# A two-block network's two expert routers: ranks in fewer products, modulation pieces at other places, values broadcast in row groups

## The reference

```python
def hier_moe(tokens, w1, b1, w2, b2, w_gate, w_up, w_down):
    p1 = jax.nn.softmax((tokens @ w1 + b1).astype(jnp.float32), axis=-1)
    p_grp, grp = lax.top_k(p1, 1)
    lg2 = (tokens @ w2 + b2).astype(jnp.float32).reshape(n, N_GROUPS, EXPERTS_PER_GROUP)
    lg2 = jnp.take_along_axis(lg2, grp[:, :, None], axis=1)[:, 0]
    top_val, top_idx = lax.top_k(lg2, TOP_K_INNER)
    gate = p_grp * jax.nn.softmax(top_val, axis=-1)
    expert = grp * EXPERTS_PER_GROUP + top_idx
    return grouped_experts(tokens, expert, gate.astype(tokens.dtype), w_gate, w_up, w_down)

sh1, sc1, g1, sh2, sc2, g2 = jnp.split(jax.nn.silu(cond) @ w + b, 6, axis=-1)   # the modulation, per layer
```

## Time and profile before

| | us |
|---|---|
| median of 3 runs | 2017.17 (2016.58 to 2017.70) |
| profiled execution, its own time | 2015.87 |
| its span | 2014.0 |
| TensorE busy in the span | 1789.0 (89%) |
| DVE, ACT, POOL busy | 1017.2, 418.1, 566.7 |
| read from HBM | 572.08 MB, 285 GB/s over the span |

### The profile page before, as it was taken

How to read it: one execution, slowest core, us unless ns; L and a number is a source line. 1 busy time by engine, 2 the same in 40 slices (tenths; PEclk the granted TensorE clock), 3 DMA queues, 4 the chain that set the end, 5 groups by cost and what they waited for, 6 DMA issues and landing times.

```text
span 2014.0 us, 56742 instructions
## 1 busy us (share of the span) xinstructions
PE 1789.0 (89%) x23884; PEld 1238.6 (61%) x23885; DVE 1017.2 (51%) x2416; ACT 418.1 (21%) x832; POOL 566.7 (28%) x431
## 2 busy tenths in 40 slices
PE   7999989999999987898988967667669989999998
PEld 4444466666666654645776745445447777788887
DVE  3798156677666656346345633333246995210001
ACT  2001242212211214115341211111113224210001
POOL 0000026777766761001033522222248000100000
PEclk9999989999999998999989987887888889999999
DMA  9854168899999999822169999999996255433320
GB/s 369 310 205 167 42 233 351 340 422 429 427 430 429 427 430 396 294 84 74 43 249 429 417 428 428 429 428 429 429 413 236 101 217 202 167 126 126 126 105 21
DMA packets 109379, 574.33 MB, mean 285 GB/s; under 512 B 4976, under 2 KB 10224, under 8 KB 84592
## 3 DMA queue, kind: packets, MB, share of 16 engines
q1 hardware_dynamic: 108720, 570.72, 70.7%
q10 hardware_dynamic: 576, 2.43, 0.3%
HBM read 572.08 MB, written 1.05 MB: 285 GB/s over the span
## 4 chain that ended last, share of the span: by engine, by line
PE 62%; DMA 26%; DVE 6%; issue 2%; ACT 2%; SPq 2%; DVEq 0%; ACTq 0%
PE bank L349 24%; PE bank L554 14%; DMA ring<-in_expert_w_gate 11%; DMA ring<-in_expert_w_down 7%; DMA ring<-in_expert_w_up 6%; PE bank L526 4%; PE bank L974 4%; PE bank L508 3%; PE bank L601 3%; DVE b L1034 2%; ACT b L1847 2%; DMA ring<-in_conv_w_in 1%; PE bank L890 1%; PE bank L420 1%; DMA ring<-in_attn_w_in 1%
## 5 line engine op out<-in xcount | busy, mean ns | idle before, releaser
L554 PE MATMUL bank<-ring,b 128*32 128x128 f32 (+1 forms) x13600 | 521.0, 310 | 133.7 <-DMA ring<-in_expert_w_gate 75.3
L554 PEld LDWEIGHTS bank<-ring,b 128*32 128x32 f32 x13600 | 402.3, 116 | 305.4 <-issue 155.1
L1034 DVE TENSOR_TENSOR h_t<-h_t,bank 128x512 f32<-128x512 f32 (+1 forms) x696 | 349.9, 564 | 316.6 <-PE bank L526 316.6
L349 PE MATMUL bank<-h_t,ring 128*128 128x256 f32 (+1 forms) x1600 | 424.0, 427 | 5.2 <-ACT h_t L1847 2.5
L1847 ACT ACTIVATE b<-bank 128x256 f32<-128x256 f32 (+4 forms) x371 | 142.8, 400 | 1298.0 <-PE bank L554 749.5
L349 PEld LDWEIGHTS bank<-h_t,ring 128*128 128x128 f32 x1600 | 306.9, 193 | 116.5 <-issue 77.4
L2269 POOL TENSOR_SCALAR b<-b 128x1024 f32<-128x1024 f32 (+1 forms) x85 | 195.1, 2295 | 46.0 <-POOL b L2277 33.6
L2277 POOL TENSOR_TENSOR b<-b 128x512 f32<-128x512 f32 (+1 forms) x85 | 88.8, 1045 | 411.5 <-PE bank L526 411.5
L526 PE MATMUL bank<-b 32*128 32x512 f32 (+1 forms) x1392 | 172.3, 565 | 5.4 <-DVE h_t L1034 4.7
L1034 DVE TENSOR_TENSOR b<-b,bank 128x128 f32<-128x128 f32 (+3 forms) x124 | 49.9, 406 | 234.4 <-PE bank L349 155.0
L2272 POOL TENSOR_TENSOR b<-b,b 128x1024 f32<-128x1024 f32 (+1 forms) x85 | 161.6, 1901 | 7.1
(11 more groups left out here) (298 smaller groups left out, 1464.0 us busy)
## 6 DMA issues: line engine op xcount, KB each, us to landing
ring<-in_expert_w_gate SPq DMA_DIRECT2D x64, 2048.0 KB, 18.7
ring<-in_expert_w_up SPq DMA_DIRECT2D x64, 2048.0 KB, 21.2
ring<-in_expert_w_down SPq DMA_DIRECT2D x64, 2048.0 KB, 21.5
ring<-in_ada_w SPq DMA_DIRECT2D x24, 2048.0 KB, 15.1
ring<-in_w_mod SPq DMA_DIRECT2D x12, 2048.0 KB, 9.1
ring<-in_w_in SPq DMA_DIRECT2D x6, 2048.0 KB, 10.5
ring<-in_w_ffn_gate SPq DMA_DIRECT2D x5, 2048.0 KB, 7.8
ring<-in_w_ffn_up SPq DMA_DIRECT2D x5, 2048.0 KB, 8.2
```

Of the source, the lines that this page charges most:

```text
L349: last = pe.matmul(o, lhs(k), rhs(k), start=(k == 0), stop=(k == nk - 1))
L554: last = pe.matmul(b[32 * m:32 * m + 32, 0:width], lhs[:, k, :], rhs[:, k, m * width:(m + 1) * width], start=(k == 0), stop=(k == nk - 1), ...
L1034: return dv.tensor_tensor(o, a, b, op)
```

## The change

Three things, in both routers.

- **Ranks.** One product per token tile with ones, whose right side is the tile's choices repeated for every later block (so the totals are added on in the same product), one triangular product for tile 0 and one for all other tiles: 6 products instead of 14 in layer 0, 4 instead of 5 in layer 1. They move 448 and 160 columns, as before.
- **Pieces.** In layer 0 piece 14 stands behind the third token group and piece 15 behind the sixth; pieces 12 to 15 are turned behind the ranks; piece 16 stands between the order's product and the bases; piece 17 stays behind the bases. In layer 1 piece 24 alone stands ahead of the logits, pieces 25 and 26 before the ranks, piece 27 behind. ACT's copies follow.
- **Values.** POOL's diagonal products go. The values' columns in `small` are placed 32 apart (`value_at`). TensorE waits for `placed`, transposes `small`, and dispatches; ACT copies the transposed bank once a tile, scaled by a mask column of `ones_m` that keeps one row in each group of 32 (`value_rows`). Four products of 32 rows, each in its own row group, give the four banks of `spread`. DVE makes the mask during the conv stage.

```diff
-ROUTER0 = (range(12, 14), range(14, 15), range(15, 18))
-ROUTER1 = (range(24, 26), (), range(26, 28))
+ROUTER0 = ((12, 13), (14, 15), (16, 17))
+ROUTER1 = ((24,), (25, 26), (27,))
...
+        value_rows = v3(b12, 6656, 4, P)
...
+        value_at = (0, 32, 20, 24, 28, 96, 64, 52)
...
-                for p in pieces[0]:
-                    turn_piece(p)
-                for p in pieces[1]:
-                    piece(p)
+                    if layer == 0 and i in (2, 5):
+                        piece(pieces[1][i // 3])
                 if layer == 1:
+                    for p in pieces[0]:
+                        turn_piece(p)
+                    for p in pieces[1]:
+                        piece(p)
                     for j in range(2):
                         turn_state_weights(j)
                 pe.wait_ge(sem(f"chosen{layer}"), 1)
...
                 def ranks(b):
-                    for t in range(tiles + 1):
-                        for s in range(min(t + 1, tiles)):
-                            tri = cn("before") if s == t else ones_c[:, :]
-                            last = pe.matmul(b[:, NE * t:NE * t + NE], tri, sel[:, s, :],
-                                             start=(s == 0), stop=(s == min(t, tiles - 1)))
+                    pe.matmul(b[:, 0:NE], cn("before"), sel[:, 0, :], start=True, stop=True)
+                    for s in range(tiles):
+                        later = tiles - s
+                        last = pe.matmul(v3(b, NE * (s + 1), later, NE), ones_c[:, :],
+                                         sel[:, s:s + 1, :].broadcast_to([P, later, NE]),
+                                         start=(s == 0), stop=(s == tiles - 1))
+                        if s == 0:
+                            pe.matmul(v3(b, NE, tiles - 1, NE), cn("before"), sel[:, 1:tiles, :], start=False, stop=False)
...
-                for p in pieces[1]:
+                for p in pieces[1] if layer else pieces[0] + pieces[1]:
                     turn_piece(p)
                 if layer == 0:
-                    piece(pieces[2][0])
                     pe.wait_ge(sem("order_ready"), 1)
                     group("v", lambda b: pe.matmul(b[:, 0:NE + 1], n_chunks[0:NE, NE:NE + 1].broadcast_to([NE, P]),
                                                    later[0:NE, :], start=True, stop=True))
+                    piece(pieces[2][0])
                     pe.wait_ge(sem("order_ready"), 2)
...
+                pe.wait_ge(sem(f"placed{layer}"), 1)
+                group("a", lambda b: transposes(b, [(0, small)]))
                 dispatch(0)
+                pe.wait_ge(a_free, lane["a"])
+                rows = value_rows.rearrange("p t n -> p (t n)")
                 for i in range(4):
-                    pe.wait_ge(sem(f"diag_ready{layer}"), i + 1)
-                    group("a", lambda b: pe.matmul(b[:, 0:ntok], ones_c[:, :], diag[i][:, 0:ntok], start=True, stop=True))
+                    group("a", lambda b: pe.matmul(b[:, 0:ntok], ones_c[32 * i:32 * i + 32, :], rows[32 * i:32 * i + 32, 0:ntok],
+                                                   start=True, stop=True, tile_position=(32 * i, 0)))
...
             fuse(0, 3, "ln1", 0)
+            do(tt(ones_m[:, 0:4], cn("iota", 0, 4), lane.broadcast_to([P, 4]), ALU.is_equal))
...
+                b = full()
+                for t in range(tiles):
+                    ins = act(value_rows[:, t, :], b[:, 0:P], ACT.Copy, scale=ones_m[:, t:t + 1])
+                taken(ins)
                 for i in range(4):
                     b = full()
                     taken(act(spread[:, i, 0:ntok], b[:, 0:ntok], ACT.Copy))
...
-                po.wait_ge(sem(f"placed{layer}"), 1)
-                g = [small[:, 4 * i:4 * i + tiles] for i in (0, 1, 6, 5)]
-                for i in range(4):
-                    po.tensor_tensor(v3(diag[i], 0, tiles, P), ident.unsqueeze(1).broadcast_to([P, tiles, P]),
-                                     g[i].unsqueeze(2).broadcast_to([P, tiles, P]), ALU.mult) \
-                        .then_inc(sem(f"diag_ready{layer}"), 1)
```

More of the change, by code:

```diff
@@ L245, in two_blocks @@
         picks, caps = v3(b3, 3456, 2, 4), v3(b3, 3464, 2, 4)
-        diag = [b12[:, 6656:7168], b12[:, 7168:7680], b3[:, 3616:4128], b3[:, 4128:4640]]
+        value_rows = v3(b12, 6656, 4, P)
         route, logit_t = v3(b3, 4640, 4, 36), b3[:, 4784:5040]
@@ L448, in moe @@
                 group("v", lambda b: transposes(b, [(P * c, logit_t[:, c * P:(c + 1) * P]) for c in range(tiles // 2)]))
-                for t in range(tiles):
-                    for half in range(2):
-                        group("a", lambda b: transposes(b, [
-                            (P * kk, H[:, 4 * half + kk, t * P:(t + 1) * P]) for kk in range(4)]))
-                for p in pieces[0]:
-                    turn_piece(p)
-                for p in pieces[1]:
-                    piece(p)
+                for i in range(2 * tiles):
+                    t, half = i // 2, i % 2
+                    group("a", lambda b: transposes(b, [
+                        (P * kk, H[:, 4 * half + kk, t * P:(t + 1) * P]) for kk in range(4)]))
+                    if layer == 0 and i in (2, 5):
+                        piece(pieces[1][i // 3])
                 if layer == 1:
+                    for p in pieces[0]:
+                        turn_piece(p)
+                    for p in pieces[1]:
+                        piece(p)
                     for j in range(2):
@@ L1118, in moe @@
                 l1, l2 = route[:, 0:tiles, 0:NG], route[:, 0:tiles, NG:36]
-                g = [small[:, 4 * i:4 * i + tiles].unsqueeze(2) for i in range(8)]
-                four = [v3(small, 32 + 16 * i, 4, NG)[:, 0:tiles, :] for i in range(4)]
+                g = [small[:, at:at + tiles].unsqueeze(2) for at in value_at]
+                four = [v3(small, 4 + 32 * i, 4, NG)[:, 0:tiles, :] for i in range(4)]
                 to4 = lambda a: a.broadcast_to([P, tiles, NG])
@@ L1930, in moe @@
                     taken(act(rows, b.rearrange("p (m q k) -> p m q k", m=2, k=KD), ACT.Copy))
+                    if layer == 0 and i in (2, 5):
+                        take_piece(pieces[1][i // 3])
                 ac.wait_ge(a_free, taken.n)
                 ac.sem_inc(copied.sem, 2 * tiles)
-                for p in pieces[0]:
-                    take_turned(p)
-                g = [small[:, 4 * i:4 * i + tiles] for i in range(8)]
-                four = [v3(small, 32 + 16 * i, 4, NG)[:, 0:tiles, :] for i in range(3)]
+                if layer == 1:
+                    for p in pieces[0]:
+                        take_turned(p)
+                g = [small[:, at:at + tiles] for at in value_at]
+                four = [v3(small, 4 + 32 * i, 4, NG)[:, 0:tiles, :] for i in range(3)]
                 ac.wait_ge(sem(f"router_shift{layer}"), 1)
@@ L1940, in moe @@
                 act(g[5], g[4], ACT.Exp).then_inc(sem(f"router_exp{layer}"), 1)
-                for p in pieces[1]:
-                    take_piece(p)
                 if layer == 1:
+                    for p in pieces[1]:
+                        take_piece(p)
                     for j in range(4):
```

## The result

| us | before | changed |
|---|---|---|
| median of 7 runs each | 2017.17 (2014.78 to 2019.91) | 2005.13 (1999.89 to 2009.62) |
| ratio, 95% interval | | 0.994, 0.9926 to 0.9954 |
| profiled execution | 2015.87 | 2007.37 |
| its span | 2014.0 | 2005.5 |
| granted clock, whole span | 0.950 | 0.954 |

The medians differ by 12.0 us, the profiled executions by 8.5. So the 0.6% belongs to the medians, and the traces say where it comes from stage by stage.

A forecast was written before the change was run, and what follows sets the result against it. TensorE and DMA were taken to bound in turns: layer 0 until 401 us by its loop's start, layer 1 by its loads. 5.6 (router) + 1.85 (broadcast) + 3.5 (layer 1) = 11 us, so 2006.2 us, range 2002.5 to 2011.5.

The forecast's parts named there:

- Step 1: Layer 0's router: pieces 14 and 15 run at full clock among the token transposes; ranks start at 281.9 instead of 284.74.
- Step 2: Layer 0's ranks: 12 instructions for 28, 1.5 us in all; counts there at 283.8 instead of 288.62.
- Step 3: Layer 0's router: DVE's order steps cover the four turned pieces; order product at 285.95, a 1.6 us wait gone.
- Step 4: Layer 0's router: piece 16 covers DVE's steps for the bases at the low clock, 3.4 us; piece 17 takes 1.9.
- The rival of low pieces: Both routers: the pieces run at the low clock, so the gain is 6 us and the time 2011.2; chance 14%.
- Step 6: Layer 0's broadcast, dispatch to first combine: 5.75 us for 7.6, a gain of 1.85, bounds 0 and 2.56.
- What the router of layer 0 gains reaches the end whole: Layer 0's expert loop: times until 401 us hang on when the loop begins, so the 7.4 us gain is kept.
- the first sign of being wrong: Layer 0's expert loop: the prediction is wrong if the stretch from 401 to 772 us gets longer.
- Layer 1: Layer 1's router: moved pieces free slots sooner, so the stream of loads begins 3.5 us earlier, bounds 1 and 5.5.
- The second sign of being wrong: Layer 1's expert loop: the prediction is wrong if its last expert ends less than 6 us earlier.
- layer 1 gives nothing: Layer 1: ranks wait behind pieces 25 and 26 and the load stream tears; gain 7.4 us, time 2009.8; chance 8%.
- the expert loop takes its gain back: Layer 0's expert loop: loads are the bound there as well; gain only 3.5 us, time 2013.7; chance 5%.

The follow-up runs named there:

- E1: Changed kernel with POOL's nine clears of the experts' sums moved behind the signal placed, in both layers; 2002.55 us, ratio 0.9937.
- E12: The same kernel as E1 once more: changed kernel with POOL's clears behind placed; 2005.27 us, ratio 0.9942.
- E6: Changed kernel with POOL's clears behind placed, layer 0's piece 16 ahead of the order's product and the four turned pieces behind it; 2002.87 us, ratio 0.9933.
- E10: The same kernel as E6 once more, beside the changed kernel on the same chip; 2002.28 us, ratio 0.9925.
- E4: Changed kernel with layer 0's pieces, turns and evictions where they stood before; 2007.24 us, ratio 0.9951.
- E3: Kernel before with the values' part alone: no diagonals, one transpose, masked copies, products in four row groups; 2015.77 us, ratio 1.0.
- E2: Changed kernel with layer 1's pieces as before: 24 and 25 ahead of the logits, 26 and 27 behind the ranks; 2011.88 us, ratio 0.9977.
- E8: Changed kernel again, no edit; 2003.65 us, ratio 0.9932.
- E11: Changed kernel again, no edit, in another job; 2005.08 us, ratio 0.9937.
- E5: Kernel before with layer 1's pieces alone moved: 24 ahead of the logits, 25 and 26 before the ranks, 27 behind; 2013.17 us, ratio 0.9985.
- E7: Kernel before with POOL's clears held back until the ranks are done, so they run beside DVE's order steps; 2017.15 us, ratio 1.0004.

## Why the forecast was right, and where it wasn't

The median came 1.1 us below the 2006.2 forecast, within the range and faster by more than 0.2%. The terms did less well.

- **Step 1, pieces 14 and 15 among the transposes: right.** Full clock, ranks from 279.22, and the counts' end at 19.23 from S where the forecast has 283.8 - 264.33 = 19.5.
- **Step 2, ranks: right**, 12 instructions in 1.4 us for 1.5.
- **Step 3 failed:** "DVE's order steps, 288.62 to 290.75, cover the four turned pieces. Order product at 285.95." Counted from S that is 21.6. E1, E12, E6 and E10 have 21.45 to 21.59; the changed kernel has 25.3, 22.8 and 25.3. The step took the duration from a stretch in which POOL had finished, and moved it to one in which POOL was clearing. The earlier trace rows had shown it: POOL busy for 2.71 of 3 us in 282 to 285.
- **Step 4, "I price it at the low clock, 3.4", piece 17 full: its reasons failed.** The rival of low pieces was half right: of the six executions of pieces 16 and 17 in three traces five were slow (3.64 four times, 2.73 once), with 2.95 to 5.48 us of idle ahead of the order's product. The rival had put it down to the clock alone; E12, E6, E10 and E4 show 1.95 each where no such idle was, though E1 (2.68 and 3.64 behind 1.64 us of idle) does not fit. The dispatch came 0.4 us later to 3.2 us earlier, counted from S, for 5.6 forecast; E12's came 7.2 earlier, the upper bound of 7.1.
- **Step 6, the broadcast: right in itself**, 1.92 us for 1.85. The combine waited 0.52 us for ACT in E12. The page of the Trainium skill that the prediction cited (TensorEngine Tiling (Array Packing), "PSUM Bottleneck") says that after such a speedup the copy may become the bottleneck. The trace agrees: the four copies, 2.06 us together, bound it. That all of it reaches the end was wrong in E3's trace.
- **"What the router of layer 0 gains reaches the end whole": not in the first chunks.** From the first combine to 401 the changed kernel needs 0.8 to 2.1 us more, most of it the stops in the expert products (0.45, 0.98 and 1.80 us); E2, the same code there, had no such stop and needs 0.4 less. The load that ends the dry stretch came 0.7 to 3.8 us earlier from S, and 6.2 in E2, for 7.4. Behind it the first sign of being wrong came: from that load to the last down product of layer 0 it is 370.48 us before and 371.94, 371.83 and 371.97 in the changed kernel. It isn't tied to the change: the other traces have 370.2 to 370.5, with the change's parts or without, and E3 371.64.
- **Layer 1: right in mechanism, short in size.** 5.1 us for 3.5. The logits ran at the full clock (1.98 us, "up to twice" was forecast), so down1's issue came 4.7 us earlier from the stage's start (17.59 for 22.28), and the stream didn't tear. Up1 was issued 8.0 us earlier in the stage; gate1, which now waits for a piece behind the logits, 4.4 later, which the prediction didn't count out. The term had also set something aside for a low piece 25, which ran at the full clock; without that its own sum was 4.2. The second sign of being wrong didn't come: the last expert of layer 1 ended 8.2 us earlier.
- **The sum** of the measured stages is 0.7 to 3.8 plus 5, some 6 to 9 us (11 with E2's layer 0). The medians have 12, in the first job as against E8 and E11. In the first pair of traces the rest is 3.5 us, where the profiled executions stood to their medians, and 2.6 ahead of the router, in code that the change hardly touches, where S scatters between 261.75 and 264.68. (One small operation of the change, the mask, does stand ahead of it; E3 has it too, and the latest S.) Whether the change has a part in that isn't settled. So the forecast's closeness is in part luck: layer 0's term was too large, layer 1's too small, and some 3 to 6 us of the medians' difference lie in no stage that the forecast counted.
- The rival "layer 1 gives nothing" fell by E5 and E2; "the expert loop takes its gain back" is true for 0.8 to 2.1 us (4.7 in E10), by another mechanism than the loads; the slower one wasn't seen. The chances of the cases add up to 0.91 for faster and 0.05 for within, where the line of chances has 0.88 and 0.08.

## What to carry to other kernels

A duration read in one place holds only beside the same neighbours: when a step moves, list what every other engine does in the time it moves into, GpSimd's clears as well as DMA, not only what it waits for. Ask also what the wait behind it does to TensorE: behind an idle of 3 to 5.5 us most of the next pieces of 64 small instructions took 3.64 us for 1.95. A part's worth is best read from intervals between fixed events, since executions lie up to 5 us from their median (8 in E2) while the parts are worth 2 to 5; and an interval wants more than one trace, since the same code of layer 0 gained from 0.7 to 6.2 us.

The best version here is E6's, which beats the kernel before by 12.6 and 14.6 us; its lead over the changed kernel, 0.8 and 2.8 us in two jobs, is less than can be told from none.

## What the hardware showed

- DVE's TENSOR_SCALAR steps of 128x33 from SBUF to SBUF in fp32 were held by POOL's MEMSETs, in two forms: one step to the last clear's end (4.02, 4.03, 2.07 us for 0.18), or several lengthened to 0.42 to 0.79 each, for 0.18 to 0.24. In the second form POOL's first eight clears took 3.93 us for 3.75 (E8). The step that read PSUM (0.19), the reduction (0.18 to 0.19), SCALAR_TENSOR_TENSOR (0.20) and, among the TENSOR_SCALARs, the one of 128x32 behind it (0.24) took what they take without the clears.
- The next piece ran at 1.2 GHz (3.64 us) behind idles of 5.47 and 5.48 us. Behind 2.95 us it took 2.73 in E8 and 3.64 in E2; behind 1.64 us 1.95 in E12 and 2.68 in E1; behind 1.54 us 1.95 in E4, but behind 1.42 us 3.51 in E7. The idle alone doesn't say what the clock will be.
- The stops in the first up product have a companion in the DMA queues. Windows of E10's transfers, the kind "instruction":

```profile
q8 instruction: 1, 0.02, 6.0%
q14 instruction: 1, 0.01, 1.9%
```

These two packets fell into 298 to 299 us, and TensorE went on at 300.58. In E11 they fell into 303 to 304, and it went on at 305.44 after 1.80; in the profiled changed kernel they came at 302 to 303, before TensorE reached that place (the product began at 303.83), and there was no stop. The place speaks for code too. E3's ranks have 28 instructions where the other kernels with the stop have 12, and in TensorE's timeline of E3 the stop stands 16 instructions earlier in the product:

```profile
306.88 0.86 PE L559 MATMUL bank<-ring,b 128*32 128x128 f32 x24
308.62 1.30 PE L559 MATMUL bank<-ring,b 128*32 128x128 f32 x40 [0.88 <-issue]
```

So TensorE probably waited for its own code behind the expert loads; that was read from the traces, not tried.
